# Last stage of a hybrid encoder layer: the last expert's rows kept on chip and added by a one-hot product

## What is computed

```python
gate = (softmax(top_v) * pg[:, None]).reshape(-1)        # two picks per token, 32 experts
for each expert e:                                       # rows gathered by token
    h = silu(xb @ w_g[e]) * (xb @ w_u[e]);  y = h @ w_d[e]
x = layer_norm(ALPHA * x + sum over the 2 picks of gate * y, ln3_g, ln3_b)
```

## Time and profile before

| | us |
|---|---|
| median of 3 runs | 1662.84 |
| lowest, highest | 1659.43, 1665.26 |
| the profiled execution | 1658.88 |
| its span | 1657.0 |

### The profile page before, as it was taken

One profiled execution on the slowest core, in us unless ns is written; L12 is line 12 of the kernel. 1 busy time (PEld: TensorE's weight loads), 2 busy tenths in 40 slices (PEclk: granted clock), 3 DMA queues, 4 the chain that ended last, 5 costly groups with the idle time before them and its releaser, 6 DMA issues.

```text
span 1657.0 us, 21516 instructions
## 1 busy us (share of the span) xinstructions
PE 1582.8 (96%) x8402; PEld 1306.0 (79%) x8402; DVE 995.5 (60%) x1315; ACT 764.7 (46%) x1089; POOL 254.0 (15%) x220
## 2 busy tenths in 40 slices
PE   8999999899998999999999988999999999999966
PEld 3578887789886788999877767888888888888852
DVE  1410211477755466122554457989998899998936
ACT  2310111444445102222422222878888788888834
POOL 0000000300017471000021111111101111111105
PEclk9999999999999999999999987999999999999988
DMA  9710211600011644300335554899999999999967
GB/s 352 247 53 32 72 57 58 235 25 20 10 65 52 233 151 179 112 26 14 127 128 174 170 178 185 335 379 383 387 393 392 393 395 390 399 394 382 360 260 293
DMA packets 84001, 351.66 MB, mean 212 GB/s; under 512 B 23346, under 2 KB 26034, under 8 KB 62020
## 3 DMA queue, kind: packets, MB, share of 16 engines
q1 hardware_dynamic: 73780, 330.43, 52.7%
q0 software_dynamic: 9216, 18.89, 3.0%
q10 hardware_dynamic: 912, 1.05, 0.2%
HBM read 321.93 MB, written 43.15 MB: 220 GB/s over the span
## 4 chain that ended last, share of the span: by engine, by line
PE 91%; ACT 3%; DVE 2%; DMA 1%; issue 1%; POOL 0%; DVEq 0%; POOLq 0%; SPq 0%; ACTq 0%
PE M L1245 27%; PE M L974 12%; PE T L780 6%; PE M L771 5%; PE T L1245 5%; PE T L714 4%; PE M L854 4%; PE T L1292 3%; PE M L714 2%; PE T L1048 2%; PE T L1046 2%; PE T L1047 2%; PE M L1080 2%; PE M L738 2%; PE M L1062 2%; PE T L1348 2%
## 5 line engine op out<-in xcount | busy, mean ns | idle before, releaser
L1747 DVE TENSOR_TENSOR rounded<-beside,rounded 128x1024 fp32r<-128x1024 f32 (+1 forms) x397 | 471.6, 1233 | 97.5 <-ACT rounded L1363 47.6
L1245 PE MATMUL M<-rounded 128*128 128x512 f32 x1920 | 467.2, 394 | 4.7 <-issue 2.5
L1245 PEld LDWEIGHTS M<-rounded 128*128 128x128 f32 x1920 | 360.3, 189 | 80.7 <-issue 2.6
L1634 ACT CAST rounded<-beside 128x1024 fp32r<-128x1024 f32 x256 | 260.0, 1051 | 77.2 <-DMA beside<-in_w_exp_up 69.5
L974 PE MATMUL M<-rounded 128*128 128x512 f32 x864 | 209.8, 398 | 3.0 <-ACT rounded L1504 1.6
L974 PEld LDWEIGHTS M<-rounded 128*128 128x128 f32 x864 | 160.5, 190 | 36.2 <-issue 2.2
L1644 ACT CAST rounded<-beside 128x1024 fp32r<-128x1024 f32 x128 | 125.7, 1050 | 26.4 <-DMA beside<-in_w_exp_down 24.1
L1747 DVE TENSOR_TENSOR rounded<-T,rounded 128x512 fp32r<-128x512 f32 (+2 forms) x98 | 92.5, 947 | 34.5 <-ACT rounded L1517 17.7
L1245 PE MATMUL T<-rounded 128*128 128x512 f32 x384 | 108.7, 398 | 0.0
L2364 POOL DMA_INDIRECT expert_rows<-beside,route_out x32 | 37.3, 1166 | 385.6 <-ACT beside L1675 368.3
L714 PE MATMUL T<-tables,arena 128*128 128x128 f32 x572 | 79.3, 282 | 15.0 <-DMA arena<-in_mem_prompt 6.8
(11 more groups left out here) (339 smaller groups left out, 2325.5 us busy)
## 6 DMA issues: line engine op xcount, KB each, us to landing
beside<-in_w_exp_gate SPq DMA_DIRECT2D x64, 1024.0 KB, 8.1
beside<-in_w_exp_up SPq DMA_DIRECT2D x64, 1024.0 KB, 11.0
beside<-in_w_exp_down SPq DMA_DIRECT2D x32, 2048.0 KB, 11.7
arena<-x_rows SPq DMA_DIRECT2D x27, 512.0 KB, 3.8
x_rows<-arena SPq DMA_DIRECT2D x18, 512.0 KB, 3.0
arena<-expert_rows SPq DMA_DIRECT2D x9, 1024.0 KB, 12.7
arena<-in_x_prompt SPq DMA_DIRECT2D x16, 512.0 KB, 4.1
arena<-in_cache_mem_k SPq DMA_DIRECT2D x8, 1024.0 KB, 5.7
```

The costliest lines, as they stand in the source:

```text
L1245: got = nc.tensor.matmul(out, x[xs], (high, low)[ws](w)[:, c:c + 512], start=(first and n == 0), stop=(last and n == 2))
L1634: nc.scalar.copy(as_both(high(c)), both_raw(c)).then_inc(gu_high, 1)
L1747: return nc.vector.tensor_tensor(out, x, highs.bitcast(f32), ALU.subtract)
```

## The change

The last expert's rows are no longer scattered. ScalarE multiplies them by their gates as it copies them (`own_gate`), and they are split into a high and a low rounded part (`y_hi` by ScalarE, `y_lo` by VectorE) in the place of `xT_parts[0]`. GpSimd builds for each tile a 128x128 block, 1 where a slot's token is the column's (`own_slot`). TensorE adds `own_slot` x `y_hi` and `own_slot` x `y_lo` to every position's sum (four matmuls of 512 columns). Its rows in `expert_rows`, which are still read, are cleared at the start of the stage by a scatter of zeros out of `xg[1]`, on which the gather for expert 1 waits. The gates go to DRAM in the order of `expert_rows` and are gathered by slot. `yk` lies elsewhere, so that the picks can be loaded once scatter 30 has landed and the last weights are split; seven x2 rows are loaded earlier, two between the picks. `SEQ` is now in plain order and `BY_PE` leaves out tiles 1 and 4, whose picks VectorE adds in place ahead of positions 0 and 3. One test `more > 0` stands around the overflow loop.

```diff
-        yk = [area(WA + (11 + 2 * t) * D, 2, D) for t in range(NT)]
-        SEQ, BY_PE = (0, 2, 1, 3, 4, 5, 6, 7, 8), (1, 3, 4, 5, 6, 7, 8)
+        yk = [area(at, 2, D) for at in (11 * D, 13 * D, 30720, 32768, 34816, 39168, 41216, 43264, 45312)]
+        SEQ, BY_PE, EARLY = (0, 1, 2, 3, 4, 5, 6, 7, 8), (0, 2, 3, 5, 6, 7, 8), 7
+        y_hi, y_lo, own_slot = rounded[:, 24 * D:25 * D], rounded[:, 25 * D:26 * D], rounded[:, 26 * D:26 * D + NT * P]
...
+                else:
+                    sp.wait_ge(kT_ready, 4 + 2 * H + 1)
+                    sp.dma_start(gates_dram.rearrange("(t p k) c -> p t (k c)", p=P, k=2), gate_rows).then_inc(edge_out, 16)
...
-            with sp.Fori(0, MORE) as i:
-                with sp.If(i < more):
+            with sp.If(more > 0):
+                with sp.Fori(0, MORE) as i:
...
+            for t in SEQ[0:EARLY]:
+                load_rows(t, ln_in)
+            sp.wait_ge(gu_low, 8 * more + 8 * NE)
+            sp.wait_ge(down_low, 4 * more + 4 * NE)
             sp.wait_ge(ye_out[1], 16 * (NE // 2))
             sp.wait_ge(ye_out[0], 16 * more + 16 * (NE // 2))
+            load_picks(SEQ[0])
+            sp.dma_start(gain3, A["ln3_g"].to_broadcast([P, D])).then_inc(mv_in, 16)
+            load_picks(SEQ[1])
+            sp.dma_start(shift3, A["ln3_b"].to_broadcast([P, D])).then_inc(mv_in, 16)
+            for n in range(2, NT):
+                load_picks(SEQ[n])
+                if n + 2 < NT and n + 2 >= 4 and n - 2 + EARLY < NT:
+                    load_rows(SEQ[n - 2 + EARLY], last_in[SEQ[n - 2 + EARLY]])
...
+            for n, t in enumerate(SEQ):
                 if n > 1:
+                    pe.wait_ge(sum_done, NORMS + n - 1)
                 out = T[n % 2]
+                if t in BY_PE:
+                    pe.wait_ge(last_in[t], 16 if n < EARLY else 32)
+                    for k in (0, 1):
+                        for c in (0, 512):
+                            nc.tensor.matmul(out[:, c:c + 512], diag[2 * BY_PE.index(t) + k], yk[t][:, k, c:c + 512], start=(k == 0), stop=False)
+                if n == 0:
+                    pe.wait_ge(pads_ready, 5)
+                    pe.wait_ge(att_high, 4 + 4 * H + 1)
+                    pe.wait_ge(kT_ready, 4 + 2 * H + 2)
+                for part in (y_hi, y_lo):
                     for c in (0, 512):
+                        got = nc.tensor.matmul(out[:, c:c + 512], own_slot[:, t * P:(t + 1) * P], part[:, c:c + 512],
+                                               start=(t not in BY_PE and part is y_hi), stop=(part is y_lo))
                 got.then_inc(picks_ps, 1)
...
+            nc.scalar.copy(y_hi, yo[1]).then_inc(att_high, 1)
...
+            def sum_picks(p):
+                t = SEQ[p]
+                dve.wait_ge(last_in[t], 16 if p < EARLY else 32)
+                then(nc.vector.scalar_tensor_tensor(xl[t], yk[t][:, 0, :], gates[:, 0, t:t + 1], xl[t], ALU.mult, ALU.add))
+                then(nc.vector.scalar_tensor_tensor(xl[t], yk[t][:, 1, :], gates[:, 1, t:t + 1], xl[t], ALU.mult, ALU.add))
...
+            sum_picks(1)
             sum_rows(0)
             for p in range(PT):
+                if p == 2:
+                    sum_picks(4)
                 sum_rows(p + 1)
...
             gather(0, 0)
+            pool.sem_inc(waited, 1)
+            nc.gpsimd.indirect_dma_start(out=ye_dram, out_offset=bass.IndirectOffsetOnAxis(ap=route_out[:, NE - 1:NE], axis=0),
+                                         in_=xg[1], in_offset=None, bounds_check=2 * NT * P - 1,
+                                         oob_is_err=False).then_inc(ye_out[1], 16)
+            pool.wait_ge(ye_out[1], 16)
             gather(1, 1)
+            pool.wait_ge(edge_out, 16 * (5 + NB))
+            pool.sem_inc(waited, 1)
+            nc.gpsimd.indirect_dma_start(out=own_gate, out_offset=None, in_=gates_dram,
...
-            for b in (NE - 2, NE - 1):
-                scatter(b, b, b % 2)
+            scatter(NE - 2, NE - 2, 0)
...
+            for t in range(NT):
+                got = nc.gpsimd.tensor_scalar(own_slot[:, t * P:(t + 1) * P], iota, own_token, float(-P * t), ALU.subtract, ALU.is_equal)
+            got.then_inc(pads_ready, 1)
```

More of the change, by code:

```diff
@@ L687, in _, with load_rows, load_picks @@
             sp.wait_ge(gu_used, 8 * more + 8 * NE)
[L688 to L691, removed]
+            def load_rows(t, landed):
+                sp.dma_start(xl[t], x2_dram[t * P:(t + 1) * P, :]).then_inc(landed, 16)
+            def load_picks(t):
+                sp.dma_start(yk[t], ye_pairs[t * P:(t + 1) * P, :, :]).then_inc(last_in[t], 16)
+            for t in SEQ[0:EARLY]:
+                load_rows(t, ln_in)
+            sp.wait_ge(gu_low, 8 * more + 8 * NE)
+            sp.wait_ge(down_low, 4 * more + 4 * NE)
             sp.wait_ge(ye_out[1], 16 * (NE // 2))
             sp.wait_ge(ye_out[0], 16 * more + 16 * (NE // 2))
-            for t in range(NT):
-                sp.dma_start(yk[t], ye_pairs[t * P:(t + 1) * P, :, :]).then_inc(last_in[t], 16)
+            load_picks(SEQ[0])
[6 more added lines that the diff above has]
+                    load_rows(SEQ[n - 2 + EARLY], last_in[SEQ[n - 2 + EARLY]])
             for n, t in enumerate(SEQ):
@@ L1324, in _ @@
             more = pe.value_load(plan[0:1, MORE:MORE + 1], min_val=0, max_val=MORE)
-            with pe.Fori(0, MORE) as i:
-                with pe.If(i < more):
+            with pe.If(more > 0):
+                with pe.Fori(0, MORE) as i:
                     b = i + NE
@@ L1671, in results @@
             def results(b, u, uses):
-                if not (isinstance(uses, int) and uses == 0):
-                    act.wait_ge(ye_out[u], 16 * uses)
+                if u == 1:
+                    act.wait_ge(ye_out[1], 16 * uses + 16)
+                elif not (isinstance(uses, int) and uses == 0):
+                    act.wait_ge(ye_out[0], 16 * uses)
                 act.wait_ge(down_used, 4 * b + 4)
@@ L2116, in _ @@
             then(nc.vector.reciprocal(gates[:, 0, :], r_den))
-            nc.vector.tensor_tensor(gates[:, 1, :], gates[:, 0, :], r_e2, ALU.mult)
+            then(nc.vector.tensor_tensor(gates[:, 1, :], gates[:, 0, :], r_e2, ALU.mult))
+            then(nc.vector.tensor_scalar(gates, gates, 1.0 / ALPHA, None, ALU.mult))
+            nc.vector.tensor_copy(gate_rows, gates.rearrange("p k t -> p t k")).then_inc(kT_ready, 1)
             for k in (0, 1):
@@ L2139, in _ @@
             nc.vector.tensor_copy(plan[0:1, 0:MORE], more_expert[0:1, :])
[L2140 removed]
+            nc.vector.tensor_scalar(plan[0:1, MORE:MORE + 1], r_end[0:1, NE - 1:NE], 0.0, float(MORE), ALU.is_gt, ALU.mult).then_inc(plan_ready, 1)
             for b in range(NE):
@@ L2161, in _ @@
             more = dve.value_load(plan[0:1, MORE:MORE + 1], min_val=0, max_val=MORE)
-            with dve.Fori(0, MORE) as i:
-                with dve.If(i < more):
+            with dve.If(more > 0):
+                with dve.Fori(0, MORE) as i:
                     b = i + NE
@@ L2185, in _ @@
                     hidden_low(b, 0)
-            then(nc.vector.tensor_scalar(gates, gates, 1.0 / ALPHA, None, ALU.mult))
             for n, t in enumerate(BY_PE):
```

53 lines of the change are left out of this document (27 added, 26 removed).

## The result

| | before | after |
|---|---|---|
| median, us | 1662.26 | 1669.61 |
| lowest, highest | 1659.38, 1668.51 | 1662.92, 1675.82 |
| the profiled execution | 1658.88 | 1669.24 |
| its span | 1657.0 | 1667.4 |

The ratio of after to before is 1.0044, with an interval of 1.0029 to 1.0058: 7.3 us slower. The prediction was 1663.3, no change, with a range up to 1669.

A forecast was written before the change was run, and what follows sets the result against it. TensorE held 91% of the chain; the end was 13.2 us idle, 26.3 us of products, 14.0 us of tail. +0.1 (end) and +0.4 (start) gave +0.5 us on the 1662.84 median: 1663.3 us, range 1658 to 1669.

The forecast's parts named there:

- Part 7: Start of the stage: clearing the last expert's rows delays the gather for expert 1; charged +0.4 us, bounds 0 and 6.6.
- rival (a): Start: gather for expert 1 comes late, TensorE stands in expert 0; +6.6 us, 1669.5 us; chance 0.13.
- the gather of own_gate has 15 us to spare: Start of the stage: this gather and the later one for expert 2 were said to have 15 us to spare.
- the lower bound of 0 for an early clear: Start of the stage: if the clear lands in 4.2 us, the added cost is 0.
- Part 4: End: VectorE adds tiles 1 and 4, two passes of 1.28 us each; position 5 starts at 1625.7, products end 1643.1.
- Part 1: End: one-hot products add four matmuls, 0.93 us a position; TensorE's work becomes 32.4 us, 8.4 more.
- Part 2: End: picks wait for scatter 30, landing at 1601.9; first pick lands at 1606.8, 7.3 us earlier.
- Part 5: Overflow loop: one test removes 8.7 us of empty turns, none on the chain; up to 2 us for the jump.
- Part 6: GpSimd's nine one-hot blocks: 0.47 us each, 4.2 us in all, nothing gained; above 0.6 us each named as wrong.
- The tail: From TensorE's last product to the span's end: the same instructions, unchanged at 14.0 us.
- the +0.1 of the sum: End of the stage: last product at 1643.1 against 1642.98 before, same tail behind it, so +0.1 us.

The follow-up runs named there:

- d: The changed kernel, with GpSimd's first multiplication by the gain waiting until VectorE has added tile 4's picks; ratio to the kernel before 1.0027.
- f: The changed kernel without the one-hot products for the seven tiles of `BY_PE` (last expert's rows missing there); one execution of 1667.52 us.
- a: The changed kernel with `own_gate`'s gather counted on a semaphore of its own; one execution of 1668.2 us.
- c_both: As a, plus zeros scattered from `shift2`, so the gather for expert 1 goes out first without waiting; ratio to the kernel before 1.0006.
- e_all: c_both plus the wait of d, counted on `plan_ready`; ratio to the kernel before 1.0000.
- g_one_test: The kernel before with only one test around the overflow loop, on all five engines; ratio to the kernel before 0.9981.
- m: g_one_test with plain tile order and tiles 2 and 5 on VectorE, no one-hot part; ratio to the kernel before 0.9993.
- n: As m, plus eleven needless full f32 products on TensorE before the first picks; ratio to the kernel before 0.9986.
- i: As h, plus twelve needless rounded products on TensorE right behind the last expert; ratio to the kernel before 0.9999.
- k: As j, plus twelve needless rounded products on TensorE ahead of the first picks; ratio to the kernel before 0.9998.
- h: e_all with gain3 and shift3 loaded behind the seven rows, the last two rows behind position 4's picks; ratio to the kernel before 1.0017.
- j: e_all with nine x2 rows, gain3 and shift3 loaded before all picks, during the last gate/up products; ratio to the kernel before 1.0005.

## Why the prediction was wrong

**Part 7 failed, in two steps, and it is the mechanism of rival (a).** First, the landing of the zeros: I took 9.3 us, measured 11.2 in after, my own upper bound, and 12.3 to 13.6 in the others with this code (d, f, a). Of the 6.6 us that stood there as the upper end, the profiled execution has 3.6, and others 4.5 (a_own_sem) and 6.9 (d and f). That the 1669.5 of rival (a) is the measured median is luck: it holds nothing for the end. I had given it 0.13, with "SP loads nothing from 1023 to 1039" against it. The writing of the gates was in that gap, and GpSimd waits for it behind the zeros. It was issued at 1026.54 and let the gather of `own_gate` go only at 1039.06, 12.5 us later, where the earlier trace rows had 3.2 us for 1024 pieces of 384 B. The Trainium skill ("DMA: Bandwidth & Descriptors", Specifications) says that below 512 B a transfer is done as read-modify-write. I had cited that and then put no price on it. No run here separates its share from the zeros'. Second, "the gather of own_gate has 15 us to spare" was wrong in kind: its count is one that `turn_rows` waits for. The code says so. It cost 0.9 us of idle time in after and 2.8 and 2.6 in d and f. With it the lower bound of 0 for an early clear was wrong as well: in after's trace the gates' way (12.5 us and 3.25) ends at 1042.3, where the turn began.

**Part 4 failed in size.** The end piece, step by step:

| us | predicted | after | off by |
|---|---|---|---|
| last expert's end to the first product | 3.35 | 2.72 | -0.63 |
| first product to position 5 | 18.9 | 21.73 | +2.83 |
| position 5 to the last product's end | 17.4 | 19.30 | +1.90 |
| end piece | 39.65 | 43.75 | +4.10 |

What sets position 5 I had right, VectorE's wait for tile 4, and f_no_onehot shows it. What failed is the price of the second pass. Of the 2.83, tile 4's picks were 0.9 late and the second pass 2.14 long; the rest went the other way by 0.2. I priced both passes at the 1.28 of the earlier trace rows, where GpSimd had nothing to do; the change moves them into the stretch where it multiplies. Of the 1.90, 0.3 is there behind short idle time as well (position 5 to the end is 17.71 in d_gain_wait) and 1.6 is the clock: I let TensorE wait 1.5 us before position 5 and put no clock on that wait. At 1.45 us none was needed (d), at 3.44 it was (after, and 2.8 us of it in c_both). The Trainium skill has the first half of it ("SBUF — State Buffer", Who interferes with whom): a VectorE instruction with two SBUF inputs contends with a GpSimd instruction that reads SBUF, and whichever begins second is blocked until the other is done. The traces agree. In after GpSimd began first and the pass ended 1.08 us behind its end, where a pass alone takes 1.28; in f_no_onehot VectorE began first, and then each blocked the other once (3.12 and 3.24); in a_own_sem only GpSimd was held up (3.09). VectorE's sums (L2241), which take one input from PSUM, keep their 1.22 us beside the same multiplication. That rule should have been a rival; it was in none of mine.

**What held.** Part 1: 0.93 us for four one-hot records. Part 2: 4.14 us for scatter 30 with the first pick 4.8 behind it, the first product within 0.7 us. Part 5: the turns were hidden, and a jump cost VectorE less than the bound of 2 us, under 0.1. Part 6: 6.78 us for nine blocks, 0.75 each. That is above the 0.6 I had named as wrong, and 1.6 times the 0.47 taken, but far below 1.87, and hidden (they end at 1611.0, TensorE asks for them at 1617.1). The tail: 14.07.

**What is left of the change.** Mended at both ends it is equal to the kernel before (e_all). The one test around the overflow loop is in it too; if the 0.9981 of g_one_test is real, the rest costs by as much. Its price of 0.93 us a position eats what the earlier picks give, which is what the +0.1 of the sum said.

## What to carry to other kernels

Before a pass is moved to another time, look at what the neighbouring engine does at that time: a duration read in a quiet stretch holds for a quiet stretch only. For every new DMA look up whose wait its semaphore is in, and what must land before it can be issued. For every wait that you allow TensorE, price the clock behind it as well as the wait. Profile more than one execution before you put a price on a piece: here the same code gave 41.4 and 43.8 us at the end, and 24.0 and 27.4 at the start. Loads that are moved earlier land on what already runs there; if that is the scatter on which the first load depends, nothing is gained.

## What the runs showed of the hardware

- A VectorE pass over 128x1024 f32 with two SBUF inputs takes 1.28 us alone. Where GpSimd's multiplication was running or took its turn first, the pass ended 1.08 to 1.09 us behind it, whenever it had begun: 3.42 us (after, c), 3.24 (f), 2.06 (m, n). GpSimd's multiplication takes 2.36 alone and 3.09 to 3.17 where VectorE's pass came first (a, f, m).
- The idle time of TensorE alone does not tell whether the clock falls. Eight records took 3.70 us or less behind 2.72 and 3.29 us of idle time with needless products ahead (i, k), and 3.67 behind 3.38 (m), but 5.37 behind 2.72 (after) and behind 2.19 (n). Nor does it tell the price: behind 3.44 us they took 5.28 (after) and 6.51 (c).
- A scatter of up to 128 rows landed in 3.2 to 3.8 us with next to nothing loaded beside it (g, n, m), in 4.0 to 5.2 where the engines still moved about 400 GB/s for its first one or two microseconds (before, after, a, c, d, e, f), in 7.0 to 7.5 where they did so for three or more (h, i, j, k), and in 11.2 to 14.0 at the start of the experts, beside 2 MB of weights and the gates' 1152 pieces (all ten runs with the change).
- On VectorE jumping over the whole overflow loop cost less than 0.1 us (g: the next instruction began at 1598.21, the one before it at 1597.08 with 1.22 us), and its 18 empty turns with a test each 8.7 us.
